# Two layers of attention and mixture of experts: plain-order upper parts, another order of expert work, and a low-rank query by rounded products

## The chip, the cores and the metric

One core of one Trainium2 chip. The time is what the device takes for one execution of the whole program, in microseconds; the figure for a kernel is the median of its runs. The engines are PE (TensorE, with PEld for its weight loads), DVE (VectorE), ACT (ScalarE), POOL (GpSimd) and SP (SyncE), which here only issues loads. TensorE's clock has two levels, 2.4 GHz (shown as 1.00) and 1.2 GHz (0.50).

## The reference

256 tokens of width 1024, in fp32, go through two layers. Layer 0: differential attention, then a mixture of experts. Layer 1: latent attention, then the experts with other weights. Cut to what matters:

```python
for layer in range(DEPTH):                      # DEPTH = 2
    if layer < 1:
        h = _diff_attention(x, diff_w_qkv[layer], ...)
    else:
        k_nope, v_shared, k_rope = _mla_shared_kv(x, mla_w_kv_a, ...)
        h = _mla_attention(x, mla_w_q_a[j], ..., k_nope, v_shared, k_rope, cos, sin)
    x = _layernorm(DEEPNORM_ALPHA * x + h, ...)
    f = _grouped_moe(x, router_w, router_b, moe_w_gate[layer], moe_w_up[layer], moe_w_down[layer])
    x = _layernorm(DEEPNORM_ALPHA * x + f, ...)

# latent attention: ranks 384 (query) and 256 (key-value), 64 rotated columns, 8 heads of 128
kv_a = x @ w_kv_a                               # 1024 x 320
c_kv = _rmsnorm(kv_a[..., :256], kv_norm_g)
k_rope = _rope(kv_a[..., 256:], cos, sin)
kv = c_kv @ w_kv_b                              # 256 x 2048
q = _rmsnorm(x @ w_q_a, q_norm_g) @ w_q_b       # 1024 x 384, 384 x 1536
q_rope = _rope(q[..., 128:], cos, sin)

# experts: 32 experts of 1024 x 256, each token goes to the 2 best of one group of 4
h = silu(t @ w_gate[e]) * (t @ w_up[e])
y = y + combine[:, e:e + 1] * (h @ w_down[e])
```

## The kernel before, in words

**Exact products from rounded ones.** A fast product takes operands rounded to a shorter form (fp32r). An fp32 product is then made of three: upper part by upper part, upper by remainder, remainder by upper. The upper part is a rounding copy; the remainder is a subtraction. Most of the work of ACT, DVE and POOL here is making these parts, moving PSUM to SBUF, and norms.

**Order.** Nothing is scheduled automatically. Each engine has its own stream in program order, written out by hand, and the streams meet at semaphores: `mq[...]` for the second attention, `m(...)` for the experts, `ring_gate0` and so on for weights that have arrived. `chain(...)` (`dve_chain`, `pool_chain`) makes an instruction wait for the one before it on its own engine.

**Weights.** Three slots of the buffer `ring` hold three pairs of experts. SP reloads a slot part by part when its pair has used it: gate and up after `gu_ps` of the pair (`reload`, L487), down after `y_ps`. During the attentions the slots hold attention weights instead.

**Experts** (`moe`, `pair` on PE, twice in the program). The tokens are sorted by expert: ACT makes the upper part of the normed tokens (`upper_part`, L1478 to L1482), PE makes the remainders from it by products with the identity and with `minus_ident` (`remainders`, L980), DVE builds the one-hot matrix (`scratch_rounded`), PE multiplies (`sort`), ACT and DVE copy the even and odd eighths out of PSUM (`sorted_copy`). Each of 16 pairs then takes a window of 64 sorted tokens for each of its two experts, copied by POOL (`windows`, L2241), for the first pair by DVE (`first_windows`, L2110). PE does gate, up, down and the return into token order (`combine_previous`). Pairs 1 to 12 do gate and up interleaved, pairs 0, 13, 14 and 15 gate first and then up, so that they need not wait for the whole load. `SORT_WAIT` is a number of filler products on zeros (`zeros_b`) ahead of the sort.

**Second attention.** SP loads `mla_w_q_a` (`qa`, L552), `mla_w_kv_a` (`kva`), `mla_w_q_b` (`qb`) and `mla_w_kv_b` (`kvb`). PE transposes the residual (`transpose_x`); ACT and DVE copy it to `xT`; PE forms the low-rank query from `qa` by 16 plain fp32 products of 128x384 (two records of the trace each) and the low-rank keys and values from `kva`. Then PE forms the rotated query columns, and groups g = 0 to 11: 0 to 3 query heads, 4 to 7 key heads, 8 to 11 values. `lower_c` (DVE, L1911) makes the remainders of the normed low-rank vectors, which PE needs for its groups (`ct_sb`). DVE rotates the keys' 64 columns and half of the queries' (`rotate`, L435 to L440: six chained instructions a call, each with two inputs in SBUF), and moves the odd groups out of PSUM (`move`, L1931 and L1934). POOL scales the residual (`scale_shift`, L2217 and L2218), subtracts for the remainders of `qb` and `kvb` (L2338, five instructions), rotates the other half of the queries, and splits a part of the output weight (`split_wo`, L2233 and L2234). After group 8 PE transposes the rotated keys and queries; it then needs the rotations of both engines and all moves of DVE (`kr_rot`, `rope_dve`, `b_dve` 4).

## Time and profile before

| | |
|---|---|
| median of 3 runs | 706.66 us (705.73 to 706.89) |
| the profiled execution | 708.07 us |
| its span | 705.6 us, mean granted clock 0.991 |
| PE busy | 674.1 us (96%), 3622 matmuls |
| PEld busy | 377.3 us (53%) |
| DVE busy | 321.4 us (46%) |
| ACT busy | 219.3 us (31%) |
| POOL busy | 125.9 us (18%) |
| DMA | 237.73 MB, mean 337 GB/s |
| chain that ended last | PE 80%, DMA 7%, DVE 6%, ACT 3% |

PE is busy nearly throughout, so the table says little about single waits; what decides is which wait ends last in each stage. Times inside the program are microseconds from the start of the span. The second attention lies at about 355 to 465, the front of the second experts at 466 to 485, their pairs from there to the end.

### The profile page before, as it was taken

How to read it: one execution, taken by the hardware profiler on the slowest of the kernel's cores; microseconds unless marked ns; L12 is line 12 of the kernel's file. 1: busy time of each engine (PE TensorE's matmuls, PEld its weight loads, DVE VectorE, ACT ScalarE, POOL GpSimd, SP SyncE). 2: the span in 40 equal slices, each digit the busy share in tenths (PEclk: the TensorE clock that was granted, in tenths of full speed). 3: DMA queues.
4: the chain of work that ended last, by engine and by line, in shares of the span. 5: the costliest groups of instructions: out<-in, count | busy, mean ns of one | idle time of the engine just before them, and what ended most of it. 6: DMA issues, size and time to landing. Idle time of an engine off the chain costs nothing.

```text
span 705.6 us, 9710 instructions
## 1 busy us (share of the span) xinstructions
PE 674.1 (96%) x3622; PEld 377.3 (53%) x3624; DVE 321.4 (46%) x665; ACT 219.3 (31%) x420; POOL 125.9 (18%) x141
## 2 busy tenths in 40 slices
PE   9999999999999999999989898999999999999993
PEld 6969878463333433445546776856333343344551
DVE  4758755743243242332274756674324324233226
ACT  4568660731111111111155136363111111111112
POOL 0404110052010100100029560005201010010000
PEclk9999999999999999999999999999999999999998
DMA  8990059879999999999995019388999999999991
GB/s 330 364 370 2 1 201 401 362 301 391 423 421 421 420 422 421 421 422 421 412 414 230 1 29 426 149 345 318 378 423 420 423 420 421 421 420 422 420 396 76
DMA packets 42285, 237.73 MB, mean 337 GB/s; under 512 B 3888, under 2 KB 4064, under 8 KB 18176
## 3 DMA queue, kind: packets, MB, share of 16 engines
q1 hardware_dynamic: 41232, 235.36, 82.1%
q10 hardware_dynamic: 576, 1.05, 0.4%
q0 software_dynamic: 432, 0.70, 0.3%
q8 instruction: 31, 0.51, 0.3%
q14 instruction: 14, 0.11, 0.0%
HBM read 236.04 MB, written 1.05 MB: 336 GB/s over the span
## 4 chain that ended last, share of the span: by engine, by line
PE 80%; DMA 7%; DVE 6%; ACT 3%; SPq 2%; issue 2%; DVEq 0%; ACTq 0%
PE psum L582 77%; DMA ring<-in_moe_w_up 4%; DMA ring<-in_diff_w_qkv 3%; PE psum L1066 1%; DVE ln_stats L1674 1%; SPq L470 1%; DVE work L435 1%; SPq L455 1%; ACT work_rounded L1481 1%; PE psum L957 1%; PE psum L905 1%; SPq L457 1%; ACT scratch L1277 0%; ACT x_res L1472 0%; PE psum L688 0%
## 5 line engine op out<-in xcount | busy, mean ns | idle before, releaser
L582 PE MATMUL psum<-ring,work 128*64 128x512 f32 (+2 forms) x1296 | 230.2, 505 | 1.8 <-DMA ring<-in_moe_w_up 1.0
L582 PEld LDWEIGHTS psum<-ring,work 128*64 128x64 f32 (+1 forms) x1296 | 94.4, 138 | 134.5 <-issue 116.1
L582 PE MATMUL psum<-ring,scratch 128*64 128x512 f32 x512 | 116.9, 598 | 2.8 <-ACT scratch L1525 2.8
L2161 DVE TENSOR_TENSOR scratch<-psum,scratch 128x256 f32<-128x256 f32 x32 | 13.6, 425 | 189.4 <-ACT scratch L1521 189.4
L2241 POOL COPY work<-work 128x512 f32 x60 | 36.9, 619 | 293.3 <-PE psum L582 289.6
L1514 ACT ACTIVATE x_T_rounded<-psum,small 128x512 fp32r<-128x512 f32 x64 | 43.8, 687 | 107.0 <-DVE scratch_rounded L2142 77.3
L1521 ACT ACTIVATE scratch<-psum 128x256 f32<-128x256 f32 x32 | 12.3, 384 | 207.7 <-PE psum L582 207.7
L582 PEld LDWEIGHTS psum<-ring,scratch 128*64 128x64 f32 x512 | 33.9, 136 | 69.0 <-issue 63.6
L582 PE MATMUL psum<-x_T_rounded,scratch_rounded 128*128 128x512 f32 x144 | 62.9, 437 | 0.9 <-issue 0.7
L582 PE MATMUL psum<-ring_rounded 128*128 128x256 f32 (+1 forms) x214 | 61.6, 309 | 0.0
L582 PE MATMUL psum<-ring_rounded,x_T_rounded 128*128 128x512 f32 x192 | 60.8, 398 | 0.0
L582 PE MATMUL psum<-x_T_rounded,ring_rounded 128*128 128x256 f32 x256 | 44.7, 285 | 0.3 <-ACT ring_rounded L1242 0.3
L582 PEld LDWEIGHTS psum<-x_T_rounded,scratch_rounded 128*128 128x128 f32 x144 | 27.2, 189 | 31.0 <-issue 27.6
L582 PEld LDWEIGHTS psum<-ring_rounded 128*128 128x128 f32 x214 | 39.6, 194 | 2.0
L582 PEld LDWEIGHTS psum<-x_T_rounded,ring_rounded 128*128 128x128 f32 x256 | 38.4, 191 | 1.5 <-ACT ring_rounded L1242 0.8
L582 PEld LDWEIGHTS psum<-ring_rounded,x_T_rounded 128*128 128x128 f32 x192 | 34.9, 188 | 7.9 <-issue 1.3
L2146 DVE SCALAR_TENSOR_TENSOR work_rounded<-psum,small,x_T_rounded 128x512 fp32r<-128x512 f32 x32 | 24.0, 751 | 27.8 <-ACT x_T_rounded L1514 27.8
L2146 DVE SCALAR_TENSOR_TENSOR scratch_rounded<-psum,small,x_T_rounded 128x512 fp32r<-128x512 f32 x32 | 24.0, 750 | 15.6 <-ACT x_T_rounded L1514 15.3
L2133 DVE SCALAR_TENSOR_TENSOR scratch<-x_T,cst 128x256 f32<-128x256 f32 x32 | 15.5, 483 | 27.3 <-PE psum L582 27.2
L1770 DVE TENSOR_TENSOR ring_rounded<-ring,ring_rounded 128x1024 fp32r<-128x1024 f32 x20 | 24.5, 1272 | 4.6 <-ACT ring_rounded L1263 4.6
L582 PE MATMUL psum<-scratch_rounded 128*128 128x512 f32 x64 | 25.3, 396 | 0.0
L582 PE MATMUL psum<-work_rounded,scratch_rounded 128*128 128x512 f32 x64 | 25.3, 396 | 0.0
(270 smaller groups left out, 833.2 us busy)
## 6 DMA issues: line engine op xcount, KB each, us to landing
ring<-in_moe_w_gate SPq DMA_DIRECT2D x64, 1024.0 KB, 16.4
ring<-in_moe_w_up SPq DMA_DIRECT2D x64, 1024.0 KB, 20.8
ring<-in_moe_w_down SPq DMA_DIRECT2D x60, 1024.0 KB, 20.3
ring<-in_diff_w_qkv SPq DMA_DIRECT2D x5, 2048.0 KB, 20.5
ring<-in_diff_w_o SPq DMA_DIRECT2D x1, 4096.0 KB, 19.1
ring<-in_moe_w_down SPq DMA_DIRECT2D x8, 512.0 KB, 23.3
ring<-in_mla_w_o SPq DMA_DIRECT2D x1, 4096.0 KB, 35.7
ring<-in_mla_w_q_b SPq DMA_DIRECT2D x1, 2304.0 KB, 23.1
```

The lines of the kernel that those rows point to most:

```text
L435: link(eng.tensor_tensor(dst[:, :, lo], src[:, :, lo], c, ALU.mult))
L455: sp.dma_start(qkv_chunk(ring, c), wq[:, :, cols]).then_inc(ld_qkv[c], 16)
L457: sp.dma_start(cst[:, P:], consts[:, P:CONSTS]).then_inc(ld_cst, 16)
L470: sp.dma_start(slot_gu(s, j)[:, u, :, :], (moe_w_gate, moe_w_up)[u][l, i * 2 + j] .rearrange("(p k) f -> p k f", k=KD)).then_inc(rings[l][ ...
L582: return pe.matmul(dst, lhsT, rhs, start=start, stop=stop, skip_group_check=True)
L1514: act.activation(y_hi[:, c * 512:(c + 1) * 512], psum[:, 4 + c, :], ACT.Copy, scale=gate_col)\
L1521: act.activation(act_s, psum[:, 6, 0:FF], ACT.Silu).then_inc(m["s_ready"], 1)
L1770: dve.tensor_tensor(qkv_chunk(ring_r, c)[:, :, cols], qkv_chunk(ring, c)[:, :, cols], w_hi[:, c % 2, :, cols], ALU.subtract).then_inc(w_lo ...
L2133: dve.scalar_tensor_tensor(out=comb, in0=key_row[:, 0, :], scalar=at_, in1=gate_row[:, 0, :], op0=ALU.is_equal, op1=ALU.mult).then_inc(par ...
L2146: dve.scalar_tensor_tensor(out=y_lo[c], in0=psum[:, 4 + c, :], scalar=gate_col, in1=y_hi[:, c * 512:(c + 1) * 512], op0=ALU.mult, op1=ALU. ...
L2161: dve.tensor_tensor(h_sb, psum[:, 6, FF:2 * FF], act_s, ALU.mult).then_inc(m["h_ready"], 1)
L2241: last = pool.tensor_copy(xg[:, buf, :, j * WIN:(j + 1) * WIN], xsT[:, :, bass.ds(a, WIN)])
```

## The change

1. **Front of the experts, twice.** ACT's upper part is written in the order of the tokens' columns (`tok_hi[t]` from `xs[:, t, :]`) and no longer regrouped by eighths. PE's products with `minus_ident` read it in that order; the sort takes every eighth column of it as its stationary operand (`tok_hi[t][:, k::KD]`). ACT makes both upper parts ahead of the lower parts. `SORT_WAIT` goes from 2 to 0.
2. **First windows.** They go from DVE to POOL, into the other of two buffers; DVE then does its four `sorted_copy` in a row. POOL does them before `diag` and the windows of pair 1.
3. **Ring, twice.** The gate of pair 0 is done in three parts instead of two, each of which releases a part of the load of pair 3's gate (`GATE_PARTS`). Pair 1 does gate first and then up; the end of its gate (`gate_ps` 4) releases the load of pair 4's gate, the end of its up (`gu_ps` 2) that of pair 4's up.
4. **Pairs 13 and 14, twice.** Their order is gate, up, first half of the return of the pair before, transposes, second half; it was gate, first half, up, second half, transposes. Pair 15 keeps its order.
5. **Second attention.** The low-rank query comes from 48 rounded products of 128x384 (`query_rank`) instead of 16 fp32 ones. POOL splits `qa` in three pieces (a CAST and a TENSOR_TENSOR of 128x1024 each) once it has arrived and the last pair of the first experts has used the ring (`gu_ps` 16). ACT makes the upper part of `xT` (`mx_hi`, four CASTs of 128x512), DVE the remainder (`mx_lo`, four TENSOR_TENSORs of 128x512). POOL's `scale_shift` comes after its rotation and ahead of `split_wo`; it was ahead of the weights' remainders.
6. **DVE in the second attention.** `lower_c` of the keys and values comes ahead of the keys' rotation; that rotation comes after `move(1)`.

The diff, cut to its core:

```diff
+GATE_PARTS = (2, 5, 8)
...
-START_WAIT, FIRST_WAIT, NORM_WAIT, TOP_WAIT, SORT_WAIT = 14, 3, (11, 0), 6, 2
+START_WAIT, FIRST_WAIT, NORM_WAIT, TOP_WAIT, SORT_WAIT = 14, 3, (11, 0), 6, 0
...
-                for part, ks in enumerate((slice(0, 4), slice(4, KD))):
-                    sp.wait_ge(*mo[l]("gate0_ps", part + 1))
+                for part, ks in enumerate(slice(a, b) for a, b in zip((0,) + GATE_PARTS, GATE_PARTS)):
+                    sp.wait_ge(*mo[l]("gate_ps", part + 1))
...
+                sp.wait_ge(*mo[l]("gate_ps", 4))
+                load_gate_up(l, 4, 1, (0,))
+                sp.wait_ge(*mo[l]("gu_ps", 2))
+                load_gate_up(l, 4, 1, (1,))
+                sp.wait_ge(*mo[l]("y_ps", 2))
+                load_down(l, 4, 1)
...
+                pe.wait_ge(mq["w_lo"], A_LO)
+                def query_rank(b, which):
+                    for t in range(TT):
+                        tok = slice(t * P, (t + 1) * P)
+                        for k in (2 * b, 2 * b + 1):
+                            if which == 0:
+                                mm(psum[:, 2 + t, 0:QR], mx_hi[:, k, tok], qa_hi[:, k, :], k == 0, False)
+                                mm(psum[:, 2 + t, 0:QR], mx_hi[:, k, tok], qa_lo[:, k, :], False, False)
+                            else:
+                                last = mm(psum[:, 2 + t, 0:QR], mx_lo[:, k, tok], qa_hi[:, k, :], False, k == KD - 1)
...
-                low_rank(2, qa, 0, QR)
-                low_rank(3, qa, 1, QR)
+                for b in range(4):
+                    pe.wait_ge(mq["x_act"], X_PARTS[b])
+                    query_rank(b, 0)
+                    pe.wait_ge(mq["x_dve"], X_PARTS[b])
+                    query_rank(b, 1)
...
-                        last = mm(banks[c], minus_ident[:, :], tok_hi[t].rearrange("p (k n) -> p n k", k=KD)[:, 64 * c:64 * c + 64, :],
-                                  False, True)
+                        last = mm(banks[c], minus_ident[:, :], tok_hi[t][:, cols[c]], False, True)
...
-                    for half, part in enumerate((tok_hi[t], tok_lo[t])):
-                        last = mm(psum[:, SORT_BANKS[k], :], part[:, k * P:(k + 1) * P], onehot_r[:, t, :],
+                    for half, part in enumerate((tok_hi[t][:, k::KD], tok_lo[t][:, k * P:(k + 1) * P])):
+                        last = mm(psum[:, SORT_BANKS[k], :], part, onehot_r[:, t, :],
...
+                        else:
+                            combine_previous(0)
+                            transpose()
+                            combine_previous(1)
...
-                    act.copy(by_eighth(tok_hi[t]), xs[:, t, :].rearrange("p (n k) -> p k n", k=KD))\
-                       .then_inc(m["hi_ready"], 1)
+                    act.copy(tok_hi[t], xs[:, t, :]).then_inc(m["hi_ready"], 1)
...
                 move(1)
+                rotate_keys()
...
-                for k in (1, 3, 5):
+                for k in range(1, KD, 2):
                     sorted_copy(k)
-                dve.wait_ge(*m("pool_prep", 2))
-                first_windows(3, slice(0, 6))
-                sorted_copy(7)
-                first_windows(4, slice(6, KD))
...
-            scale_shift()
+            pool.wait_ge(*mo[0]("gu_ps", PAIRS))
+            pool.wait_ge(ld_qa, 16)
+            flat_hi, flat, flat_lo = (a.rearrange("p k n -> p (k n)") for a in (qa_hi, qa, qa_lo))
+            for n in range(A_LO):
+                cols = slice(n * 1024, (n + 1) * 1024)
+                chain(pool.tensor_copy(flat_hi[:, cols], flat[:, cols]))
+                pool.tensor_tensor(flat_lo[:, cols], flat[:, cols], flat_hi[:, cols], ALU.subtract).then_inc(mq["w_lo"], 1)
             for n, (w, hi, lo) in enumerate(b_parts):
                 pool.wait_ge(mq["w_hi"], n + 1)
                 pool.tensor_tensor(lo, w, hi, ALU.subtract).then_inc(mq["w_lo"], 1)
             pool.wait_ge(mq["qr_raw"], 2)
             rotate(pool, chain, qr_rot[:, 1, :, :], qr_raw[:, 1, :, :], 1, rope_tmp2, HEADS)\
                 .then_inc(mq["qr_rot_pool"], 1)
+            scale_shift()
             pool.wait_ge(mq["b_ps"], 4)
             pool.wait_ge(*scaled(x_dve, 0))
             split_wo()
```

The order on DVE in the second attention, from the copy of the second tokens' raw key columns (`kr_raw`, COPY 128x64) on. Before:

```order
L1905 COPY work<-psum 128x64
L435 TENSOR_TENSOR work<-work,cst 128x32 [waits dve_chain]
L436 TENSOR_TENSOR scratch<-work,cst 128x32 [waits dve_chain]
L437 TENSOR_TENSOR work<-work,scratch 128x32 [waits dve_chain]
L438 TENSOR_TENSOR work<-work,cst 128x32 [waits dve_chain]
L439 TENSOR_TENSOR scratch<-work,cst 128x32 [waits dve_chain]
L440 TENSOR_TENSOR work<-work,scratch 128x32 [waits dve_chain]
...
L1924 COPY work<-work 128x2x64 [waits dve_chain]
L1911 SCALAR_TENSOR_TENSOR ring_rounded<-psum,kv_norm_g_sb,scratch_rounded 128x256 [waits mla_c_hi] x2
L1931 TENSOR_SCALAR work<-psum 128x512 [waits mla_b_ps]
L435 TENSOR_TENSOR x_T<-x_T,cst 128x8x32 [waits mla_qr_raw]
```

And now:

```order
L1950 COPY work<-psum 128x64
L1956 SCALAR_TENSOR_TENSOR ring_rounded<-psum,kv_norm_g_sb,scratch_rounded 128x256 [waits mla_c_hi,dve_chain]
L1956 SCALAR_TENSOR_TENSOR ring_rounded<-psum,kv_norm_g_sb,scratch_rounded 128x256 [waits mla_c_hi]
L1980 TENSOR_SCALAR work<-psum 128x512 [waits mla_b_ps]
L446 TENSOR_TENSOR work<-work,cst 128x32
...
L1973 COPY work<-work 128x2x64 [waits dve_chain]
L446 TENSOR_TENSOR x_T<-x_T,cst 128x8x32 [waits mla_qr_raw]
L447 TENSOR_TENSOR scratch<-x_T,cst 128x256 [waits dve_chain]
...
L1980 TENSOR_SCALAR work<-psum 128x512 [waits mla_b_ps]
L1983 COPY work<-psum 128x512 [waits mla_b_ps] x2
```

The remainders `ckv_lo` (ring_rounded) and the first move pass the keys' twelve rotation instructions and their COPY; these now stand directly ahead of the six of the queries and of the moves of groups 3, 5 and 7.

The order on POOL, from the end of the first experts on. Before:

```order
L2217 TENSOR_TENSOR x_res<-x_res,ring 128x1024 [waits ld_ln,xt_ps,ln_norm]
L2218 TENSOR_TENSOR x_res<-x_res,ring 128x1024 [waits pool_chain]
L2338 TENSOR_TENSOR ring_rounded<-ring,ring_rounded 128x1536 [waits mla_w_hi] x3
L2338 TENSOR_TENSOR ring_rounded<-ring,ring_rounded 128x2048 [waits mla_w_hi] x2
L435 TENSOR_TENSOR x_T<-x_T,cst 128x8x32 [waits mla_qr_raw]
...
L440 TENSOR_TENSOR x_T<-x_T,work 128x8x32 [waits pool_chain]
L2233 CAST ring_rounded<-ring 128x1024 [waits ld_wo,x_scaled_dve,mla_b_ps]
L2234 TENSOR_TENSOR ring_rounded<-ring,ring_rounded 128x1024 [waits pool_chain]
```

And now:

```order
L2386 CAST work_rounded<-ring 128x1024 [waits ld_qa,moe_gu_ps]
L2387 TENSOR_TENSOR ring_rounded<-ring,work_rounded 128x1024 [waits pool_chain]
...
L2390 TENSOR_TENSOR ring_rounded<-ring,ring_rounded 128x1536 [waits mla_w_hi] x3
L2390 TENSOR_TENSOR ring_rounded<-ring,ring_rounded 128x2048 [waits mla_w_hi] x2
L446 TENSOR_TENSOR x_T<-x_T,cst 128x8x32 [waits mla_qr_raw]
...
L451 TENSOR_TENSOR x_T<-x_T,work 128x8x32 [waits pool_chain]
L2253 TENSOR_TENSOR x_res<-x_res,ring 128x1024 [waits ld_ln,xt_ps,ln_norm]
L2254 TENSOR_TENSOR x_res<-x_res,ring 128x1024 [waits pool_chain]
L2269 CAST ring_rounded<-ring 128x1024 [waits ld_wo,x_scaled_dve,mla_b_ps]
```

Three pairs of splitting instructions stand in front, and the two of `scale_shift` have moved from the front to between the rotation and `split_wo`.

## Rows read from the trace of the kernel before

**Rows 1.** Page, section 2: GB/s that the DMA engines moved, in 40 equal slices.

```profile
GB/s 330 364 370 2 1 201 401 362 301 391 423 421 421 420 422 421 421 422 421 412 414 230 1 29 426 149 345 318 378 423 420 423 420 421 421 420 422 420 396 76
```

**Rows 2.** Chain that ended last, in order of time: start us, us, what.

```profile
397.46 13.21 PE psum L582 x90
```

**Rows 3.** Timeline, ACT, front of the second MoE: start us, us, engine, line, operation.

```profile
466.60 2.06 ACT L1481 CAST work_rounded<-x_res 128x1024 fp32r<-128x1024 f32 x1
```

**Rows 4.** Timeline, PE, front of the second MoE.

```profile
468.70 1.34 PE L582 MATMUL psum<-work_rounded,minus_ident 128*128 128x512 f32 x2
469.97 0.28 PE L582 MATMUL psum<-ones_b,work 128*32 128x128 bf16 x2
474.52 3.55 PE L582 MATMUL psum<-x_T_rounded,work_rounded 128*128 128x512 f32 x14
```

**Rows 5.** Timeline, DVE, front and first windows of the second MoE.

```profile
468.80 0.30 DVE L2010 TENSOR_TENSOR work<-work 128x128 f32<-128x128 f32 x1
472.63 0.75 DVE L2081 SCALAR_TENSOR_TENSOR x_T_rounded<-scratch,small,x_T_rounded 128x512 fp32r<-128x512 f32 x1
481.87 0.63 DVE L2110 COPY work<-work 128x384 f32 x2 [0.23 <-DVE work L2102]
```

**Rows 6.** Groups by line, busy us, mean ns, idle before.

```profile
L2241 POOL COPY work<-work 128x512 f32 x60 | 36.9, 619 | 293.3 <-PE psum L582 289.6 <-issue 0.8
L1263 ACT CAST ring_rounded<-ring 128x1024 fp32r<-128x1024 f32 x20 | 19.8, 1051 | 9.2 <-DMA ring<-in_diff_w_qkv 9.2
```

**Rows 7.** Timeline, PE, pairs 12 to 14 of the second MoE.

```profile
638.04 7.09 PE L582 MATMUL psum<-ring,work 128*64 128x512 f32 x32 [0.96 <-DMA ring<-in_moe_w_up]
650.91 3.62 PE L582 MATMUL psum<-ring,work 128*64 128x256 f32 x32
664.83 3.62 PE L582 MATMUL psum<-ring,work 128*64 128x256 f32 x32
```

**Rows 8.** Timeline, SP: when it issued loads.

```profile
334.45 8.61 SPq L552 DMA_DIRECT2D ring<-in_mla_w_q_a  x1
...
484.55 2.10 SPq L501 DMA_DIRECT2D ring<-in_moe_w_gate  x2
502.48 0.86 SPq L470 DMA_DIRECT2D ring<-in_moe_w_gate  x2
```

**Rows 9.** DMA issues: KB each, us from issue to landing.

```profile
ring<-in_mla_w_q_a SPq DMA_DIRECT2D x1, 1536.0 KB, 20.7
```

**Rows 10.** Timeline, PE, second attention.

```profile
365.37 14.87 PE L582 MATMUL psum<-ring,x_T 128*128 128x384 f32 x48
397.46 0.39 PE L582 MATMUL psum<-scratch_rounded,ring_rounded 128*128 128x256 f32 x1 [3.40 <-DVE ring_rounded L1911]
```

**Rows 11.** Timeline, DVE, second attention.

```profile
368.91 3.28 DVE L1718 TENSOR_TENSOR x_res<-x_res,ring 128x1024 f32<-128x1024 f32 x1
386.92 4.50 DVE L435 TENSOR_TENSOR work<-work,cst 128x32 f32<-128x32 f32 x1
392.14 0.19 DVE L437 TENSOR_TENSOR work<-work,scratch 128x32 f32<-128x32 f32 x1
398.31 0.41 DVE L435 TENSOR_TENSOR x_T<-x_T,cst 128x256 f32<-128x256 f32 x1
```

**Rows 12.** Timeline, POOL, second attention.

```profile
371.05 20.32 POOL L2338 TENSOR_TENSOR ring_rounded<-ring,ring_rounded 128x1536 fp32r<-128x1536 f32 x5
392.14 0.80 POOL L436 TENSOR_TENSOR work<-x_T,cst 128x256 f32<-128x256 f32 x1
403.59 1.04 POOL L2233 CAST ring_rounded<-ring 128x1024 fp32r<-128x1024 f32 x1 [7.34 <-PE psum L582]
404.71 2.40 POOL L2234 TENSOR_TENSOR ring_rounded<-ring,ring_rounded 128x1024 fp32r<-128x1024 f32 x1
```

**Rows 13.** Windows: window, length; busy us of PE, PEld, DVE, ACT, POOL; PE clock; DMA; GB/s.

```profile
392.00:396.00 4.00, 2.06 (x18) 1.85 (x16) 3.73 (x9) 0.54 (x1) 3.61 (x6) 1.00 0.00 0
396.00:404.00 8.00, 6.54 (x42) 6.54 (x43) 5.20 (x14) 0.60 (x1) 0.66 (x2) 0.79 0.00 0
```

116 lines of the change are left out of this document (67 added, 49 removed).

## The prediction

> **What bounds the kernel now.** I read the page first. PE is busy for 674.1 of 705.6 us, and three quarters of the chain that ended last are its products; in the stretches where pairs of experts run, the DMA engines move 420 GB/s as well [rows 1]. Both limits count there. A steady pair costs PE 12.9 us: pair 12, interleaved, starts its gate and up at 638.04, pair 13 its gate at 650.91. Ahead of pair 12 stands one wait of 0.96 us for a load [rows 7]. A pair's weights are 6 loads of 1.05 MB, 6.3 MB, and at 421 GB/s they take 14.9 us. So loads lose 2 us on PE with each pair and catch up only by their head start; what PE gains early in a stage is cut off where the loads have no slack left. Next I read the chain in the second attention: after PE stood for 3.4 us it ran groups 2 to 8 as one block of 90 products, 397.46 to 410.67 [rows 2]. Then the timelines of the engines there, for who releases PE, and the windows for its clock.
>
> **Front of the experts, layer 1 (the second).** The upper part costs ACT 2.06 us [rows 3]; a copy of the same size in plain order takes 1.05 [rows 6]: 1.0 less. The two products with `minus_ident` take 1.34 us for 512 columns each in the strided form, while 14 products of the sort with 512 columns take 3.55 us, 0.25 each [rows 4]: 0.51 for the two, 0.8 less each time. The counting product at 469.97 stands behind the first two; its input was ready from DVE at 469.10 (468.80 + 0.30 [rows 5]), so it can come 0.9 earlier, or 1.07 with the shorter tail of the products; I take 1.0. DVE's first one-hot matrix ends at 473.38 (472.63 + 0.75 [rows 5]) and follows the count: 472.3 to 472.4. On PE the second two of the products with `minus_ident` come 1.8 earlier and get 0.8 shorter, and the filler goes, so PE is free before that. The sort starts at 472.4 and not at 474.52: **-2.1**. Against it the first windows cost 0.63 on DVE for both [rows 5] and 0.62 each on POOL [rows 6], the last two of them after the last sorted copy: +0.3. Net **-1.8**. The sort's stationary operand is now strided for half of its products. The nearest case is the strided residual in the transposes, whose load hides behind the product before it; I take 0, and +0.4 for each of 16 products, +6 per layer, as the bad end. In the first layer the same edits act with the filler at a low clock; I take -2.2, with +-0.6.
>
> **Ring and pairs.** Pair 1 in two parts works on 128x256 tiles twice and gains nothing; +0.1 per layer for the additional switch. Pairs 13 and 14 get the transposes between the halves of the return. Pair 13 takes 13.92 us, 650.91 to 664.83 [rows 7], a steady one 12.9: PE transposes `h` last there and must then wait for the copy (`ht_sb`) before down; in the interleaved pairs the second half of the return lies between and covers that copy, as it now does here. -1.0 each, **-1.9** per layer. The loads: the first load of pair 3's gate was issued at 484.55, 2.0 us after pair 0's start; with the first part done after two of eight slices it goes at 1.1. Pair 4's gate was issued at 502.48 [rows 8]; with pair 1 split it goes some 3.5 us earlier, and until then the rates fell to about 350 of 420 GB/s. Together the stream of loads gets about 1.9 us ahead. In the second layer the gain is capped by it: slack of the last pair 0.4, plus 1.9, plus the 1.8 by which the first issue comes earlier: **-4.1** at most, and -1.8 + 0.1 - 1.9 - 0.96 (the wait that disappears) = -4.6 without the cap. First layer: -2.2 + 0.1 - 1.9 = **-4.0**. Experts in both layers: **-8.1**.
>
> **Second attention, up to the groups.** `qa` is issued at 334.45 and lands 20.7 us later [rows 8, 9], at 355.15. POOL's three pieces, 3 x (1.04 + 2.40) by the same shapes in `split_wo` [rows 12] = 10.4, end at 365.7. The fp32 query products start at 365.37; with those of the first keys' tile they take 14.87 for 48 records, 32 of them the query's, so about 10.5 [rows 10]. The 48 rounded ones of 384 columns take 48 x 0.19 = 9.1 or less, but begin 1.1 us later, behind ACT's four additional CASTs. The saved 0.5 to 1.5 us is not seen at the end: ACT's CASTs of `qb` and `kvb` start 1.4 us later too, and the norm behind them releases the transposes of the query at 380.07 before. I take -0.2. POOL: what it gains by doing `scale_shift` later it spends on `qa`; L2338 starts at 371.45 instead of 371.05 [rows 12] and ends at 392.0.
>
> **The wait that goes.** PE's stall of 3.40 us [rows 10] ends with `ckv_lo` on DVE. That stood behind the keys' rotation, whose first instruction of 128x32 took 4.50 us, from 386.92 [rows 11], where an unobstructed one takes 0.19 [rows 11]. It ended together with POOL's L2338 at 391.37 [rows 12]. The same is seen at 368.91, 3.28 us [rows 11], until POOL's `scale_shift` ended. The one kind of DVE instruction that suffers has both inputs in SBUF; those with a PSUM input run beside POOL. With `lower_c` first (one input in PSUM) the stall is gone, and with it the low clock behind it: the clock over 396 to 404 is 0.79 [rows 13], that is 3.4 us at 1.2 GHz, 1.7 lost. Group 8 would end at 410.67 - 3.4 - 1.7 - 0.2 = **405.4**.
>
> **The wait that comes.** DVE now has twelve key rotations and their COPY, then six query rotations, then moves 3, 5 and 7, and PE needs all of it before it transposes. It starts on the keys at about 394.7, after `move(1)`. From the list of POOL: rotation until 396.9, `scale_shift` 2 x 2.40 to 401.8, `split_wo` 4 x (1.04 + 0.08 + 2.40) to 416 or 417.5. Before, POOL was idle from 396.25 until 403.59 (7.34 [rows 12]), and DVE's query rotations ran in that gap at 0.41 each [rows 11]. Now there is no gap: 18 instructions (and a COPY) of DVE with two SBUF inputs stand against about 13 of POOL, most of them 1.04 to 2.40 long. How many get through per instruction of POOL: during POOL's rotation (0.80 each [rows 12]) nine of DVE's stand beside six of POOL's from 392 to 396 [rows 13], 1.5 to 1: between two chained POOL instructions there are 0.08 us, and one that slips in there takes 0.19 [rows 11]. Where POOL does not wait between two, one gets through. I take four in the rotation's rest, then one per instruction plus one more at half of the five chained gaps: 12 or 13 in ten instructions. The rest runs when POOL ends: rotations done at about 418, plus three moves of 0.68 = 420. PE resumes at **420.0** instead of 410.5: **+9.5**. It has then stood for 14.6 us, and after a stall of 3.4 the clock already fell, so **+1.7** again.
>
> The Trainium skill, page "SBUF — State Buffer", section "Who interferes with whom", has a rule for this: of a VectorE instruction with two SBUF inputs and a GpSimd instruction that reads SBUF, whichever comes first holds the shared port pair for the whole instruction, and the other blocks. The row of 4.50 us agrees; taken strictly it gives the second rival below.
>
> **Sum.** -8.1 + 9.5 + 1.7 = +3.1 (the -0.2 lies inside the stretch before 405.4). Against the profiled execution of 708.07 that is 711.2; that execution lies 1.4 above the median of 706.66, so **709.8**. With the doubts on the first layer (0.6), the ring (1) and DVE's turns (2) this case runs from 707 to 713.
>
> **Rivals.**
> (a) *DVE gets through.* If two instructions of DVE pass with each of POOL's, all 18 are done in nine, at about 414, PE resumes at 416: -4 against my sum, 705.8, slightly faster or the same. If the block is really only an effect of long POOL instructions of L2338's kind and the rotations run at their own speed, DVE ends at 394.7 + 12 x 0.23 + 6 x 0.45 + 2 = 402, PE goes on at 405.4: -5.1 - 8.1 = -13.2, **693.5**. For it: 0.19 in the gaps. Against it: 3.28 beside a `scale_shift` of the same form. The point: PE resumes before 417. Chance 0.29, most of it in the part above 697.
> (b) *One for one.* Each instruction of DVE waits for one whole instruction of POOL. Then 15 are left at 396.9, ten pass by 417, five are done behind: rotations at 419.8, PE at 421.8: +1.8, **711.6**. The page named above asks for this one. Chance 0.18.
> (c) *The experts give less.* The loads cap both layers at the slack they had, or strided stationary reads cost: the -8.1 shrinks to -4, 713.9. For it: 420 GB/s throughout. Against it: the earlier issues. Chance 0.12.
> (d) *The split of `qa` is late*, PE waits for POOL ahead of the query: `qa` landing at 358 instead of 355 gives +3 there. Rows 9 put it just in time. Chance 0.05, about 712.
>
> My own case has 0.36. Faster by over 0.2% (1.4 us, about what a measurement of this kernel can tell from no change), that is below 705.2: (a)'s larger part and a bit of mine, where the experts give more than 8: **0.30**. Within: 0.13. Slower, above 708.1: 0.57. The range: 714 at the top takes in (b), (c) and (d); 698 at the bottom takes in most of (a). Mine alone: 707 to 713.
>
> **What would show it.** In the trace after: DVE's L446 to L451 with 128x32 of 1 to 2.4 us each instead of 0.19, ending with POOL's L2253, L2254, L2269 and L2270; an idle time of PE of 10 to 15 us behind group 8, ended by DVE; the clock at 0.50 behind it; no stall ahead of group 2; both fronts some 2 us shorter, pairs 13 and 14 at 12.9. Wrong would be: PE goes through to the transposes before 412, or experts' stages that shrink by less than 2 us each.

## The result and the profile after

| | before | after |
|---|---|---|
| median | 706.66 us | 710.92 us (709.89 to 714.04, 5 runs) |
| ratio to before | | 1.0064 (1.0045 to 1.0082) |
| the profiled execution | 708.07 us | 710.2 us |
| its span, mean clock | 705.6 us, 0.991 | 708.5 us, 0.984 |
| PE busy | 674.1 us, 3622 matmuls | 668.0 us, 3698 |
| DVE, POOL busy | 321.4, 125.9 us | 332.4, 138.5 us |

The change makes the kernel slower by 0.64%, 4.5 us (3.2 to 5.8). PE does 6 us less work and waits 9 us more. Laid beside the trace of before, the loss has one place. The norm's transposes at the end of the first experts start 3.5 us earlier (362.66 before, 359.19 after); the transposes of the residual behind the second attention 6.9 us later (460.19, 467.13); the span ends 2.9 us later. So the first experts give 3.5 us, the second attention takes 10.4, the second experts give 4.0.

What bounds the second attention now, in PE's timeline (start us, us, engine, line, operation, and in brackets the idle time before it with what ended it). It answers to [rows 10]:

```profile
415.10 0.66 PE L893 MATMUL psum<-cst,work 128*128 128x128 f32 x2 [13.14 <-DVE work L1983]
```

The wait of 3.40 us ahead of group 2 is gone, and PE stands for 13.14 us behind group 8. The releaser is the last of DVE's moves. DVE's timeline, against [rows 11] (the first row runs across the gap between two of POOL's short instructions, 391.28 to 391.36; the row at 395.46 starts with POOL's second `scale_shift` and still takes 0.19; the other rows stand beside long ones, the last comes when POOL is done):

```profile
391.14 0.19 DVE L446 TENSOR_TENSOR work<-work,cst 128x32 f32<-128x32 f32 x1
...
393.10 2.32 DVE L451 TENSOR_TENSOR work<-work,scratch 128x32 f32<-128x32 f32 x1
395.46 0.19 DVE L446 TENSOR_TENSOR work<-work,cst 128x32 f32<-128x32 f32 x1
395.69 2.28 DVE L447 TENSOR_TENSOR scratch<-work,cst 128x32 f32<-128x32 f32 x1
398.00 0.95 DVE L448 TENSOR_TENSOR work<-work,scratch 128x32 f32<-128x32 f32 x1
398.98 2.45 DVE L449 TENSOR_TENSOR work<-work,cst 128x32 f32<-128x32 f32 x1
...
402.67 2.25 DVE L1973 COPY work<-work 128x128 f32<-128x128 f32 x1
...
406.13 2.44 DVE L447 TENSOR_TENSOR scratch<-x_T,cst 128x256 f32<-128x256 f32 x1
...
412.73 0.42 DVE L451 TENSOR_TENSOR x_T<-x_T,scratch 128x256 f32<-128x256 f32 x1
```

And POOL's, against [rows 12]:

```profile
392.98 2.40 POOL L2253 TENSOR_TENSOR x_res<-x_res,ring 128x1024 f32<-128x1024 f32 x1
395.46 2.46 POOL L2254 TENSOR_TENSOR x_res<-x_res,ring 128x1024 f32<-128x1024 f32 x1
397.87 1.03 POOL L2269 CAST ring_rounded<-ring 128x1024 fp32r<-128x1024 f32 x1
398.98 2.40 POOL L2270 TENSOR_TENSOR ring_rounded<-ring,ring_rounded 128x1024 fp32r<-128x1024 f32 x1
...
409.55 2.40 POOL L2270 TENSOR_TENSOR ring_rounded<-ring,ring_rounded 128x1024 fp32r<-128x1024 f32 x1
```

Read them side by side. POOL's first `scale_shift` ends at 395.38, and DVE's L451, issued at 393.10, at 395.42. The second ends at 397.92, DVE's L447 at 397.97. The CAST ends at 398.90, L448 at 398.95. That goes on to 412: a DVE instruction which takes 0.19 us alone is recorded at 0.95 beside a CAST and at 2.3 to 2.5 beside a TENSOR_TENSOR. Of DVE's instructions from 393.10 on, ten are held to the end of one of POOL's ten, and two slip through in 0.19.

The clock, in the windows view (window, length; busy us of PE, PEld, DVE, ACT, POOL; PE clock; DMA share; GB/s), against [rows 13]:

```profile
400.00:412.00 12.00, 1.96 (x11) 1.35 (x10) 11.79 (x8) 0.00 (x0) 11.71 (x7) 0.76 0.00 0
412.00:416.00 4.00, 0.90 (x5) 0.93 (x6) 3.09 (x7) 0.00 (x0) 0.00 (x0) 0.50 0.00 0
416.00:424.00 8.00, 8.00 (x38) 6.45 (x37) 3.95 (x9) 3.41 (x7) 0.00 (x0) 0.75 0.00 0
```

The clock was 1.00 up to 400, while PE ran groups 2 to 8. It falls while PE stands, and PE resumes at 0.50, 1.2 GHz.

The front of the second experts, ACT and PE, against [rows 3] and [rows 4]:

```profile
473.53 1.05 ACT L1523 CAST work_rounded<-x_res 128x1024 fp32r<-128x1024 f32 x1
```

```profile
474.97 1.03 PE L599 MATMUL psum<-work_rounded,minus_ident 128*128 128x512 f32 x2
479.41 3.75 PE L599 MATMUL psum<-x_T_rounded,work_rounded 128*128 128x512 f32 x14
```

The two products with `minus_ident` take 1.03 us, not the 0.51 I had worked out, but they are not what the sort waits for. From ACT's upper part to the start of the sort there were 7.92 us (466.60 to 474.52), now 5.88 (473.53 to 479.41). Before, PE stood for ACT ahead of the down products of pairs 13 and 14:

```profile
661.35 3.65 PE L582 MATMUL psum<-ring,scratch 128*64 128x512 f32 x16 [0.46 <-ACT scratch L1525]
```

The chain after has no such wait in these pairs (start us, us, what):

```profile
651.01 12.56 PE psum L599 x88
664.05 12.56 PE psum L599 x88
```

### The profile page after: what moved, and what is told of

Read it like the earlier page. It is cut to its first block, busy times and chain, and to the rows that moved or that the text cites. A ratio compares the mean times of both kernels' runs of the same rounds, so it can differ in the third digit from the quotient of the medians.

```text
span 708.5 us, 9872 instructions
## 1 busy us (share of the span) xinstructions
PE 668.0 (94%) x3698; PEld 386.0 (54%) x3700; DVE 332.4 (47%) x661; ACT 217.6 (31%) x424; POOL 138.5 (20%) x155
## 3 DMA queue, kind: packets, MB, share of 16 engines
q10 hardware_dynamic: 576, 1.05, 0.4%
HBM read 236.04 MB, written 1.05 MB: 335 GB/s over the span
## 4 chain that ended last, share of the span: by engine, by line
PE 72%; SPq 10%; DVE 7%; DMA 7%; ACT 2%; issue 1%; POOL 0%; DVEq 0%; POOLq 0%; ACTq 0%
PE psum L599 68%; DMA ring<-in_mla_w_kv_b 4%; SPq L481 4%; DMA ring<-in_diff_w_qkv 3%; SPq L534 2%; SPq L486 2%; PE psum L1096 1%; DVE scratch L447 1%; PE psum L988 1%; PE psum L936 1%; SPq L466 1%; ACT ring_rounded L1417 1%; SPq L468 1%; ACT scratch L1319 0%; SPq L569 0%
## 5 line engine op out<-in xcount | busy, mean ns | idle before, releaser
L599 PEld LDWEIGHTS psum<-ring,work 128*64 128x64 f32 (+1 forms) x1360 | 99.4, 138 | 129.8 <-issue 105.3
L599 PE MATMUL psum<-ring_rounded 128*128 128x256 f32 (+2 forms) x230 | 66.8, 310 | 0.0
L599 PEld LDWEIGHTS psum<-ring_rounded 128*128 128x128 f32 x230 | 42.1, 192 | 2.1
L2182 DVE SCALAR_TENSOR_TENSOR scratch_rounded<-psum,small,x_T_rounded 128x512 fp32r<-128x512 f32 x32 | 24.0, 750 | 13.3 <-ACT x_T_rounded L1555 12.8
```

Source lines behind the costliest of these rows:

```text
L599: return pe.matmul(dst, lhsT, rhs, start=start, stop=stop, skip_group_check=True)
L2182: dve.scalar_tensor_tensor(out=y_lo[c], in0=psum[:, 4 + c, :], scalar=gate_col, in1=y_hi[:, c * 512:(c + 1) * 512], op0=ALU.mult, op1=ALU. ...
```

## The experiments

Each is told with its ratio to the kernel before on the same chip and the interval of 95%; the median stands beside it. The changed kernel has 1.0064.

### 1. POOL stands back

```diff
+            pool.wait_ge(mq["rope_dve"], 1)
             scale_shift()
             pool.wait_ge(mq["b_ps"], 4)
```

> POOL waits, behind its own rotation, until DVE has done its rotations (rope_dve), and only then scales the residual and splits the output weight. Theory (DVE and POOL exclude each other, one whole POOL instruction per DVE instruction with two SBUF inputs): DVE's 19 instructions run at 0.19 and 0.41 us instead of up to 2.46, its moves end at about 399, PE goes from group 8 straight to the transposes at about 402.3 (415.1 in the changed kernel), and the low clock behind the stall goes too, 2 us more: 710.9 - 12.8 - 2 = about 696. Rival 1 (DVE's rotations are late of themselves, since they stand behind the first move): the wait only adds, 711 or more. Rival 2 (what POOL does later is needed soon): the stall goes but 3 to 5 us come back at the output weight, 699 to 701.

Measured: **0.9869** (0.9854 to 0.9885), 698.34 us. One wait on an engine that is not on the path takes off 12.6 us by the medians, 13.8 by the ratios. DVE's rotations, in the same instructions:

```profile
394.28 0.19 DVE L446 TENSOR_TENSOR work<-work,cst 128x32 f32<-128x32 f32 x1
...
395.64 0.23 DVE L1973 COPY work<-work 128x128 f32<-128x128 f32 x1
395.78 0.42 DVE L446 TENSOR_TENSOR x_T<-x_T,cst 128x256 f32<-128x256 f32 x1
...
398.07 0.43 DVE L451 TENSOR_TENSOR x_T<-x_T,scratch 128x256 f32<-128x256 f32 x1
```

And POOL's, which stands back for 4.60 us:

```profile
393.17 0.80 POOL L451 TENSOR_TENSOR x_T<-x_T,work 128x256 f32<-128x256 f32 x1
398.58 2.41 POOL L2253 TENSOR_TENSOR x_res<-x_res,ring 128x1024 f32<-128x1024 f32 x1 [4.60 <-DVE x_T L451]
```

They are done at 398.5, PE has no wait behind group 8, and its clock stays at 1.00 from 392 to 408. Rival 1 falls. The median is 2.3 us above the 696 of the theory, near what rival 2 names, though the place is another: not the output weight, but the heads' loop. From the transposes behind group 8 to those of the residual PE takes 52.70 us here (402.59 to 455.29) and took 49.68 before (410.51 to 460.19). One part is DVE's scaling of the probabilities, which POOL's later `split_wo` now stands beside. The groups of the stretch 396 to 460, first of this kernel, then of the changed one (count, then busy us, mean ns):

```profile
L2026 DVE TENSOR_SCALAR scratch<-scratch,small 128x128 f32<-128x128 f32 x8 | 3.8, 472 | 0.0
L2026 DVE TENSOR_SCALAR scratch<-scratch,small 128x256 f32<-128x256 f32 x8 | 3.6, 445 | 0.0
```

```profile
L2026 DVE TENSOR_SCALAR scratch<-scratch,small 128x128 f32<-128x128 f32 x8 | 2.2, 278 | 0.0
L2026 DVE TENSOR_SCALAR scratch<-scratch,small 128x256 f32<-128x256 f32 x8 | 2.8, 346 | 0.0
```

2.4 us more for the same 16 instructions, and PE stands once for them, 1.33 us at 417.59, where the kernel before has no wait. The other 1.7 us are the clock, which is at 0.50 in this execution from about 428 to 431.3 (windows view, this kernel):

```profile
428.00:431.00 3.00, 3.00 (x12) 2.73 (x12) 1.28 (x7) 1.54 (x5) 0.00 (x0) 0.50 0.98 404
```

The traces of runs 6 and 7 have the same attention code, their clock is 1.00 from 424 to 436, and the stretch takes 51.01 and 50.58 us. So the low clock is not in every execution; what decides it is open.

### 2. scale_shift back in front

```diff
+            scale_shift()
             for n, (w, hi, lo) in enumerate(b_parts):
...
                 .then_inc(mq["qr_rot_pool"], 1)
-            scale_shift()
```

> The changed kernel with POOL's two scale_shift instructions back ahead of the weights' remainders (after the split of qa). Theory: ten POOL instructions behind the rotation become eight, PE resumes some 4.8 us earlier, at about 410.5: 706 to 707. Against it stands what the two do in front: 4.8 us of POOL beside DVE's four subtractions for mx_lo, each of which can be held for 2.4; PE's query products then end up to 2 us later, which the copies of qb and kvb on ACT may hide. Rival (the number of POOL instructions behind the rotation doesn't matter): PE resumes at 415 as in the changed kernel, 711.

Measured: **0.9979** (0.9967 to 0.9991), 705.58 us, 0.4 below the theory's 706, with PE resuming at 410.94. But the way there differs. In front the two instructions held DVE for more than I had allowed:

```profile
363.06 4.76 DVE L1629 TENSOR_TENSOR work_rounded<-x_T,ring_rounded 128x512 fp32r<-128x512 f32 x2 [0.48 <-ACT ring_rounded L1255]
368.65 2.59 DVE L1629 TENSOR_TENSOR work_rounded<-x_T,ring_rounded 128x512 fp32r<-128x512 f32 x2
371.16 4.54 DVE L1762 TENSOR_TENSOR x_res<-x_res,ring 128x1024 f32<-128x1024 f32 x1
```

PE's two waits in this kernel:

```profile
381.59 1.54 PE L829 MATMUL psum<-cst,work 128*128 128x128 f32 x6 [2.85 <-DVE work L1947]
...
410.94 0.41 PE L893 MATMUL psum<-cst,work 128*128 128x128 f32 x2 [2.44 <-DVE work L1983]
```

The first two rows are the four subtractions for `mx_lo` (1.56 and 1.46 in the changed kernel), the third half of DVE's own `scale_shift` (1.22 there). DVE's norm of the query is 5 us late, and PE stands 2.85 us for it ahead of the query's transposes. Behind group 8 it stands only 2.44, since it arrives there 6 us later (408.50 instead of 401.96). And DVE meets less of POOL there: POOL is idle for 3.60 us until 401.42, the keys' rotations pass at 0.19 each from 397.67 on, and only four of the queries' are held (1.30, 2.51, 1.14, 2.50), so the theory's eight instructions in the way were four. By the ratios the run gains 6.0 us, and part of what was gained behind is paid in front: at neither place is DVE free of POOL.

### 3 and 4. The two halves of the change

Parts 1 to 4 alone (both experts' stages), and parts 5 and 6 alone (the second attention). The edits are those of the change, line by line; in short, what run 3 leaves as it was and run 4 takes:

```diff
-                pe.wait_ge(ld_qa, 16)
+                pe.wait_ge(mq["w_lo"], A_LO)
...
+                rotate_keys()
...
-            scale_shift()
+            pool.wait_ge(*mo[0]("gu_ps", PAIRS))
+            pool.wait_ge(ld_qa, 16)
...
+            scale_shift()
```

> Parts 1 to 4 of the change alone, both experts' stages; the second attention as before. Theory: the two stages give what the traces show, 3.5 us in the first and 4.1 in the second: 706.66 - 7.6 = about 699. Rival (loads cap the sum): the gain of the first stage is lost again where the attention's weights arrive, 702 to 703. Rival 2: the parts gain nothing by themselves, 706 to 707.

Measured: **0.9921** (0.9907 to 0.9936), 701.61 us, between the theory and the first rival, nearer to the rival.

> Parts 5 and 6 alone, the experts' stages as before. Theory: the attention costs what the traces show between the end of the first experts and the start of the last ones, 6.9 + 3.5 = 10.4 us: about 717. Rival (the stall exists only since the first experts end earlier and the loads come later against it): 706 to 710.

Measured: **1.0131** (1.0116 to 1.0147), 716.78 us; PE stands for 13.11 us behind group 8, again for the last of DVE's moves.

The two add up: -5.6 and +9.3 us make +3.7, the change has +4.5 (3.2 to 5.8). The stall needs nothing of the experts' stages, so the rival of 4 falls. The experts' parts give 5.6 us (4.5 to 6.6) in timed runs, less than the 7.6 that the two profiled executions show. Single executions differ there (run 3's own span is 6.0 us shorter than that of before): the pairs of the first layer took 214.91 us before and 213.58 after from the first gate to the norm's transposes, but 213.95 in the trace of run 3, and 216.39 in that of run 4, which has the old order and a wait of 1.26 us for a load. Loads decide that, and one trace of each is no mean.

### 5. The rounded query

On top of run 1, 16 fp32 products again, and none of the splits of `qa` and `xT`:

```diff
-                for b in range(4):
-                    pe.wait_ge(mq["x_act"], X_PARTS[b])
-                    query_rank(b, 0)
-                    pe.wait_ge(mq["x_dve"], X_PARTS[b])
-                    query_rank(b, 1)
+                for t in range(TT):
+                    for i, k in enumerate((0, 2, 1, 3, 4, 6, 5, 7)):
...
+                        last = mm(psum[:, 2 + t, 0:QR], xT[:, k, t * P:(t + 1) * P], qa[:, k, :], i == 0, i == KD - 1)
```

> The version in which POOL waits for DVE's rotations (698.3), with the low-rank query by 16 fp32 products again, and so without POOL's split of qa, ACT's four and DVE's four additional instructions. Theory: the rounded query gives nothing, since the copies of qb and kvb on ACT and the norm behind them release PE next, and they start later with it: 698.3 within 0.7. Rival (48 rounded products save what they save on PE, 2 to 3 us): 700.5 to 701.5. Rival 2 (the late split, at which PE stood 1.5 us, makes it a loss): 697.

Measured: **0.9861** (0.9839 to 0.9882), 697.63 us: by the intervals the same as run 1 (0.9869), within some 2 us either way. The rounded query, with 14 instructions on three other engines, is worth nothing that these runs can tell. The time leaves open rival 2, by which the rounded query costs about 1 us. The traces speak against it: from the norm's transposes to the query's PE takes 17.43 us here, 17.25 in the changed kernel and 17.41 before, so the rounded products gain the 0.2 at that point. The remaining difference of the two traces lies in the heads' loop, 51.76 us here against 52.70. In the changed kernel the rounded query even begins with a wait for its own operand, and ends behind a queue on ACT:

PE's and ACT's timelines there:

```profile
363.36 0.44 PE L599 MATMUL psum<-work_rounded,ring_rounded 128*128 128x384 f32 x1 [1.54 <-POOL ring_rounded L2387]
...
376.44 0.87 PE L829 MATMUL psum<-cst,work 128*128 128x128 f32 x6 [0.18 <-DVE work L1947]
```

```profile
365.93 8.01 ACT L1417 CAST ring_rounded<-ring 128x1536 fp32r<-128x1536 f32 x5
```

ACT copies `qb` and `kvb` until 373.9 and only then takes the squares of the query's rank, which PE had ready at 371.8; PE passes the time with the keys' products.

### 6. The order of pairs 13 and 14

```diff
-                        if i == PAIRS - 1:
+                        if i > 1:
                             combine_previous(0)
...
-                        elif i == PAIRS - 1:
+                        elif i > 1:
                             combine_previous(1)
                             transpose()
```

> The same version with pairs 13 and 14 in their old order (both halves of the return ahead of the transposes). Theory: 1.0 us for each of four pairs comes back, 702.2. Rival (the loads bound the end of the experts' stages, so the order is worth little): 698.3 to 699.5, with waits of PE for loads that get shorter by what the order adds.

Measured: **0.9904** (0.9886 to 0.9923), 700.23 us, against 0.9869 of run 1. The order is worth some 2.5 us for both layers, with an uncertainty of 1.7, between theory and rival. In this trace pairs 13 and 14 take 27.68 us together in either layer, from gate to gate, and in the changed kernel's 26.05 and 25.90: there the order gives 1.6 and 1.8. In run 1's own trace they take 26.82 and 26.70, since PE waits in them, 0.18 us for a load of up (329.84) and 0.35 us ahead of pair 15's gate in the first layer, and in the second:

```profile
670.17 3.67 PE L599 MATMUL psum<-ring,work 128*64 128x256 f32 x32 [0.40 <-issue]
```

For the last two waits the profile names no releaser. The kernel with the old order has no wait for loads in these pairs; its waits for loads come earlier, 0.17 us at 300.38 and 0.52 us at 630.20. So the order gives most of its size in a trace without waits for loads, and the rival holds in part.

### 7. The releases of the ring

```diff
-GATE_PARTS = (2, 5, 8)
+GATE_PARTS = (4, 8)
...
-                sp.wait_ge(*mo[l]("gate_ps", 4))
-                load_gate_up(l, 4, 1, (0,))
-                sp.wait_ge(*mo[l]("gu_ps", 2))
-                load_gate_up(l, 4, 1, (1,))
-                sp.wait_ge(*mo[l]("y_ps", 2))
-                load_down(l, 4, 1)
-                for i in range(5, PAIRS - 1):
+                for i in range(4, PAIRS - 1):
...
-                    pair(i, i < 2 or i > LOADED_TURNS * SLOTS)
+                    pair(i, i == 0 or i > LOADED_TURNS * SLOTS)
```

> The same version with the releases of the ring as they were: pair 0's gate in two parts, pair 1 interleaved, pair 4's loads after gu_ps 2. Theory (loads are close behind PE at pair 12; the earlier releases give the stream 1.9 us of head start): PE waits again for up loads of pairs 11 to 15, 1 to 2 us in each stage, 700.5 to 702. Rival (PE had slack): 698.1, since the split of pair 1 costs 0.1 per stage.

Measured: **0.9882** (0.9859 to 0.9906), 698.40 us, against 0.9869. The intervals overlap widely. In the second layer PE waited three times for loads of up, 0.73 us at pair 12, 0.22 at 659.26 and 0.19 at 674.26, together 1.14 us, the low end of the theory for one stage; in the first layer it waited for none. By the ratios this part is worth 0.9 us with an uncertainty of 2, and the run cannot tell it from nothing.

### 8. The same work of POOL in halves

In the changed kernel, each of POOL's ten long instructions cut in two of 512 columns (shown for `split_wo`; `scale_shift` likewise):

```diff
+                    for a in (0, 512):
+                        c = slice(a, a + 512)
+                        chain(pool.tensor_copy(wo_hi(wo_b, h)[:, c], wo(ring, wo_b, h)[:, c]))
+                        last = pool.tensor_tensor(wo(ring_r, wo_b, h)[:, c], wo(ring, wo_b, h)[:, c], wo_hi(wo_b, h)[:, c], ALU.subtract)
+                        if a:
+                            last.then_inc(w_pool_ready, 1)
+                        else:
+                            chain(last)
```

> The changed kernel (710.9), with POOL's two scale_shift instructions and the eight of split_wo each cut in halves of 512 columns, interleaved in the same order and chained, so that POOL does the same work in twice as many instructions. Theory (a DVE instruction with two SBUF inputs waits for the end of one whole POOL instruction): each wait halves, 0.6 and 1.25 us instead of 1.0 and 2.4, the 14 instructions behind POOL's rotation take some 12 us instead of 20, PE resumes at about 408: 703 to 704. Rival (DVE gets a fixed share of time beside POOL): PE resumes at 415 or later, 711 or more.

Measured: **0.9992** (0.9980 to 1.0005), 706.51 us, 3 above the theory and by the ratios 5.1 below the changed kernel. POOL does the same work, in a little more time (1.35 us for half of what took 2.40), and DVE gets through faster, which speaks against the rival:

```profile
394.69 0.19 DVE L448 TENSOR_TENSOR work<-work,scratch 128x32 f32<-128x32 f32 x1
394.91 1.17 DVE L449 TENSOR_TENSOR work<-work,cst 128x32 f32<-128x32 f32 x1
396.12 0.19 DVE L450 TENSOR_TENSOR scratch<-work,cst 128x32 f32<-128x32 f32 x1
396.34 1.17 DVE L451 TENSOR_TENSOR work<-work,scratch 128x32 f32<-128x32 f32 x1
...
404.07 1.37 DVE L448 TENSOR_TENSOR x_T<-x_T,scratch 128x256 f32<-128x256 f32 x1
405.47 0.72 DVE L449 TENSOR_TENSOR x_T<-x_T,cst 128x256 f32<-128x256 f32 x1
```

POOL's timeline beside it:

```profile
394.68 1.35 POOL L2256 TENSOR_TENSOR x_res<-x_res,ring 128x512 f32<-128x512 f32 x1
396.11 1.35 POOL L2255 TENSOR_TENSOR x_res<-x_res,ring 128x512 f32<-128x512 f32 x1
```

PE waits 6.70 us and goes on at 410.28.

A held instruction costs 1.2 and not 2.4. With 128x32 tiles DVE passes two instructions with each of POOL's (1.17 and 0.19); with 128x256 tiles only one. Those six take 6.6 us; I had not counted that the larger ones win no turn. The rotations take 15.6 us (392.75 to 408.33), where the changed kernel has 22.0 (391.14 to 413.15).

### 9. Two long instructions instead of ten

```diff
             scale_shift()
+            pool.wait_ge(mq["rope_dve"], 1)
             pool.wait_ge(mq["b_ps"], 4)
```

> The changed kernel with POOL's wait for DVE's rotations behind scale_shift, ahead of split_wo: two of the ten long POOL instructions still stand beside DVE. Theory (one DVE instruction per POOL instruction): two or three waits of up to 2.4 us, DVE's rotations end about 4.8 us later than with no POOL beside them (398.4 there), at 403, its last moves at 405, and PE stands for some 2 to 3 us: 698.3 + 2.5 and up to 1.5 for the clock, 701 to 702. Rival (it takes the whole series to hurt): 698.5.

Measured: **0.9889** (0.9874 to 0.9904), 700.22 us, 0.8 below the theory's range and above the rival. The interval overlaps a little with that of run 1 (0.9854 to 0.9885), so the rows decide. DVE shows exactly two long waits, then runs free:

```profile
394.73 2.33 DVE L451 TENSOR_TENSOR work<-work,scratch 128x32 f32<-128x32 f32 x1
397.09 2.44 DVE L446 TENSOR_TENSOR work<-work,cst 128x32 f32<-128x32 f32 x1
399.57 0.19 DVE L447 TENSOR_TENSOR scratch<-work,cst 128x32 f32<-128x32 f32 x1
```

PE stands for 2.09 us, and goes on at 405.51. With ten the wait is 13.14, with two 2.09, with none nothing: the wait follows the number of POOL's instructions in DVE's way, each by its length.

### 10 and 11. The order of DVE

The keys' rotation ahead of the remainders again, on top of run 1:

```diff
-                lower_c(KVR // P, QR // P, ckv_lo, ckvT, 6, kvg)
...
+                rotate_keys()
+                lower_c(KVR // P, QR // P, ckv_lo, ckvT, 6, kvg)
...
-                rotate_keys()
```

> The version in which POOL waits for DVE's rotations (698.3), with the keys' rotation ahead of the remainders of the keys and values again (part 6 undone). Theory: DVE's first rotation is held by POOL's last long subtraction, the remainders come 3 to 4 us late, PE stands in front of group 2 for 3.4 us as before the change and the clock falls behind it: 698.3 + 3.4 + 1.7 = 703.4. Rival (the order of DVE matters only as long as POOL is in the way behind it too): 698.3.

Measured: **0.9908** (0.9891 to 0.9924), 701.98 us, against 0.9869 of run 1: 2.8 us, where 5.1 were expected. The wait and the low clock behind it (0.61 in 392 to 400) are there in full:

```profile
394.79 0.58 PE L599 MATMUL psum<-scratch_rounded,ring_rounded 128*128 128x256 f32 x1 [3.50 <-DVE ring_rounded L1956]
```

PE reaches the transposes at 408.91 instead of 402.59, 6.3 us later, and 3.0 of these come back by the residual's transposes (455.29, 458.62). The heads' loop begins later against `split_wo`: the scalings take 5.6 us and not the 7.4 of run 1, PE does not stand the 1.33 us for them, and the low clock that cost 1.7 us in the loop of run 1's trace is not there (1.00 from 424 to 436).

And part 6 alone in the kernel before:

```diff
-                for t in range(TT):
...
                 lower_c(KVR // P, QR // P, ckv_lo, ckvT, 6, kvg)
+
+                def rotate_keys():
...
                 move(1)
+                rotate_keys()
```

> The kernel before with part 6 alone (remainders of keys and values ahead of the keys' rotation). Theory: the stall of 3.4 us ahead of group 2 goes, group 3 ends earlier, and with it POOL's split_wo starts at about 399, before DVE has done its query rotations, so three or four of its instructions hold DVE; PE goes on at 408.5 instead of 410.5: about 704.5. Rival (no stall comes in its place): 706.5 - 5.1 = 701.4.

Measured: **1.0006** (0.9992 to 1.0021), 708.03 us. The wait ahead of group 2 goes, `split_wo` starts at 399.13 and stands beside the queries' rotation:

```profile
399.58 1.14 DVE L436 TENSOR_TENSOR scratch<-x_T,cst 128x256 f32<-128x256 f32 x1
400.76 2.52 DVE L437 TENSOR_TENSOR x_T<-x_T,scratch 128x256 f32<-128x256 f32 x1
...
407.01 1.14 DVE L440 TENSOR_TENSOR x_T<-x_T,scratch 128x256 f32<-128x256 f32 x1
```

PE's timeline:

```profile
410.09 0.66 PE L862 MATMUL psum<-cst,work 128*128 128x128 f32 x2 [3.88 <-DVE work L1938]
```

The mechanism is the expected one; PE goes on at 410.09 and not at 408.5; 0.7 of that is this execution's later start of the attention. The clock falls behind this wait too (0.57 in 408 to 416), which the forecast of 704.5 left out: the old loss is only moved.

### 12. Towards a faster version

Run 5 with `scale_shift` where it was before the change:

```diff
+            scale_shift()
             for n, (w, hi, lo) in enumerate(b_parts):
...
             pool.wait_ge(mq["rope_dve"], 1)
-            scale_shift()
```

> The version with fp32 query (697.6 against 706.3), with POOL's scale_shift back where it was before the change, ahead of the weights' remainders; POOL still waits for DVE's rotations ahead of split_wo. Theory: split_wo then ends 4.8 us earlier, at about 411 instead of 416, and holds only the first of DVE's probability scalings (TENSOR_SCALAR from SBUF to SBUF, 0.8 and 1.0 us there where a free pair takes 0.54): up to 1 us less, 697. In front, scale_shift stands beside DVE's own scaling of the residual as before the change, off PE's path: nothing. Rival (in front it costs, as it did beside the four subtractions of mx_lo): PE stands for DVE's norm of the query, 699 to 700.

Measured: **0.9861** (0.9840 to 0.9881), 696.25 us. The ratio is that of run 5, and the runs cannot tell the two apart. DVE's scalings of 128x128 were held more, not less (4.4 us for the eight against 3.0; one row, 410.46, has 2.77 for two beside POOL's 2.38 at 410.51). But PE no longer stands for them: the wait of 0.49 us that run 5 has at 416.23 is gone, and the clock is 1.00 throughout the loop, where run 5's is 0.50 from 427 to 429 and run 1's was low as well. From the transposes behind group 8 to the residual's PE takes 49.70 us, as before the change, against 51.76 in run 5. One trace of each shows this; the timed runs do not. Both versions are 1.4% faster than the kernel before and 2% faster than the changed one. Of the change they hold the experts' parts and part 6, and add one wait; run 5 keeps the new place of `scale_shift` as well.

## Why the prediction was right

It gave 709.8 and the median is 710.92; the sum of +3.1 for the execution stands against +2.1 in the profiled one, +2.9 in its span and +4.3 in the medians (+4.5 by the ratio, 3.2 to 5.8, so the sum lies just below the interval). By its steps, in the frame of before (after's times plus the 3.5 that PE is early, 3.6 behind the query):

- **The wait that comes**, forecast +9.5 with PE resuming at 420.0: it resumed at 415.10 + 3.6 = 418.7, +8.2. DVE began the keys at 391.14 + 3.6 = 394.7, as forecast. "12 or 13 in ten instructions" were 12: ten held, two through in 0.19. The rotations ended at 416.8 instead of 418. Runs 1, 8 and 9 change the number and length of POOL's instructions and nothing of DVE's, and the wait follows each time.
- **The clock**, forecast +1.7: from the resumption to the first softmax transposes it took 11.0 us before (410.5 to 421.5) and 13.3 after (415.1 to 428.4), +2.3. I had taken the cost behind a stall of 3.4 us for that behind one of 13, where PE begins at 1.2 GHz at once. Wait and clock together are 10.5, against 11.2.
- **The wait that goes**: gone. Group 8 ended at 401.96 + 3.6 = 405.6, forecast 405.4.
- **The query**, forecast -0.2: -0.16 (380.07 to 376.44, less the 3.47 from before). Run 5 does not contradict it. POOL's split ended at 363.3 and PE stood 1.54 us for it; rival (d) was there in small, and hidden by the same queue on ACT that hides the gain. (Its price of 3 on 709.8 makes 712.8, not the 712 given.)
- **Front**, second layer, forecast -2.1 to the start of the sort: -2.04. From there to the first gate it forecast +0.3 and measured +0.68 (8.04 to 8.72): the strided stationary operand was taken at nothing and is not quite that. The sort's first 14 products, half of them with the strided operand, take 3.75 us where they took 3.55 [rows 4]: 0.03 for each strided one. The whole sort takes 8.06 us (479.41 to 487.47) where it took 7.63, +0.43; the other 0.25 are the wait for the first windows, 0.66 instead of 0.41 and now on POOL, near the +0.3. Net -1.4 instead of -1.8.
- **Pairs and loads**, second layer, forecast -2.8 and capped to a total of -4.1: -2.77 for the pairs (211.37 to 208.60 from first gate to the last norm's statistics), total -4.1. First layer -3.5 instead of -4.0. In timed runs both give 5.6 and not 8.1; the term was too large by 2.5 us, and run 6 puts a part of that on pairs 13 and 14, whose -1.9 per layer is worth about 1.2. The cap by loads was argued for the second layer alone. Of the ring's part run 7 shows no more than 0.9 us with an uncertainty of 2.

So the step that was mis-sized is the experts' -8.1, 2.5 us too large. Wait and clock were 0.7 too large on the other side by the traces. In timed runs the attention alone costs 9.3 where 11.2 stood in the sum, 1.9 too much. The mechanism was right in both places; that the two sizes erred in opposite directions and nearly cancel, so that +3.1 comes so near to +4.5, is luck.

Rival (a) had 0.29 and falls by the rows: nothing got through two at a time for the larger tiles. Rival (b), one for one, had 711.6, and the median lies between it and my case, somewhat nearer to (b): the time does not decide between them. The rows do. Ten of the twelve instructions that passed obeyed (b), two slipped through and two were left for the end; (b) had none slip through and five left.

The rule of the Trainium skill, page "SBUF — State Buffer", section "Who interferes with whom", that whoever comes first holds the shared port pair for its whole instruction, agrees with the rows of the changed kernel and with run 8, where half the length of POOL's instructions made half the wait (1.17 against 2.45).

## What to carry to other kernels

An engine at 20% of the span can still be what the kernel waits for: ask not how busy POOL is but how long its single instructions are and what stands on DVE at the same time. Short, chained DVE work with both operands in SBUF belongs where POOL is idle or runs short instructions, and a semaphore that lets the unhurried engine stand back gave 1.9% here, net of the 1.33 us that its later work cost PE in the heads' loop. When a reorder removes a stall, look at where the work that was moved comes to lie: part 6 alone removed a wait of 3.4 us and was worth nothing.

## What the runs showed that I had not expected

- **A copy with one input is held too.** The prediction says that the one kind of DVE instruction that suffers has both inputs in SBUF. The COPY of 128x128 fp32 from SBUF to SBUF (L1973) took 2.25 us beside POOL, and 0.23 alone. The probabilities' TENSOR_SCALAR, SBUF to SBUF, was held as well (pairs of 1.56 and 1.86 us against 0.54). Moves with a PSUM input ran beside POOL at their usual 0.69 (390.53 in the changed kernel, 406.43 before). The Trainium skill's page "SBUF — State Buffer" says in the same section, "Who interferes with whom", that copies, casts and `tensor_scalar` can take the shared pair too, in their two-port modes. The rows agree in that the two are held; in which mode they ran no row shows. The prediction had left this out.
- **POOL is held back a little in turn.** Its CAST of 128x1024 took 1.03 to 1.05 elsewhere, and 1.23 at 408.25 in the changed kernel, 1.31, 1.24 and 1.23 in run 11, each time beside one of DVE's 128x256 rotations.
- **Kernels with the long wait may vary more, which is not shown.** The range is 709.89 to 714.04 after (5 executions) and 706.16 to 711.25 in run 11 (11), against 697.56 to 699.35 in run 1 (4). But the kernel before, whose only long wait there is the 3.40 us ahead of group 2, ranges from 705.08 to 709.23 in 17 executions beside run 5. The cause is open.
